# Moving the down-weight loads of a 32-expert MoE layer from SyncE's queue to GpSimd's

## The reference

```python
logits = h @ w_router + b_router                 # 32 experts
top_val, top_idx = lax.top_k(logits, 4)          # each row goes to 4 of them
gates = softmax(top_val)
...
gu = xblk @ w_gate_up[e] + b_gate_up[e]          # (rows, 1024) @ (1024, 2048)
x_glu, x_lin = split(gu); clamp both to 7
act = x_glu * sigmoid(1.702 * x_glu) * (x_lin + 1)
y = act @ w_down[e] + b_down[e]                  # (rows, 1024) @ (1024, 1024)
x[row] += gate * y
```

## Time and profile before

| | before |
|---|---|
| median of 3 runs | 1299.44 us (1299.43 to 1299.75) |
| profiled execution, its own time | 1303.46 us |
| span of the profiled execution | 1301.6 us |
| TensorE busy | 1231.7 us, 95% of the span |
| DMA, share of 16 engines, queue of SyncE (q1) | 80.0% of the span, 428.65 MB |
| DMA, queue of GpSimd (q0) | 0.6%, 3.08 MB |
| mean granted TensorE clock | 0.975 of full speed |

### The profile page before, as it was taken

The page is one execution under the profiler, slowest core; times in us unless marked ns, Lnnn a source line. Parts: engine busy times, 40 slices in busy tenths (PEclk is TensorE's granted clock), DMA queues, the critical chain, the costliest instruction groups (busy, mean ns, idle before and its releaser), DMA issues.

```text
span 1301.6 us, 15662 instructions
## 1 busy us (share of the span) xinstructions
PE 1231.7 (95%) x5923; PEld 596.5 (46%) x5923; DVE 396.1 (30%) x777; ACT 210.9 (16%) x394; POOL 78.6 (6%) x81
## 2 busy tenths in 40 slices
PE   6999979998999999999999999999999999998996
PEld 3666669856543434434343434434343443433342
DVE  3989633224342121321212121321212212121214
ACT  2134435223001101010110100001000000100002
POOL 1100144154000000000000000000000000000000
PEclk9989989798899999999999999999999999999998
DMA  9411210016999999999999999899999999999994
GB/s 378 167 69 70 87 25 2 9 49 260 397 382 421 420 422 422 422 422 422 422 422 422 422 422 422 355 361 420 422 422 421 422 422 421 421 422 420 421 422 176
DMA packets 62149, 433.69 MB, mean 333 GB/s; under 512 B 7744, under 2 KB 8128, under 8 KB 11968
## 3 DMA queue, kind: packets, MB, share of 16 engines
q1 hardware_dynamic: 59696, 428.65, 80.0%
q0 software_dynamic: 800, 3.08, 0.6%
q10 hardware_dynamic: 1616, 1.45, 0.3%
HBM read 428.50 MB, written 4.65 MB: 333 GB/s over the span
## 4 chain that ended last, share of the span: by engine, by line
PE 70%; DMA 19%; SPq 6%; DVE 2%; issue 1%; ACT 0%; ACTq 0%
PE bank L1718 20%; DMA ring<-in_w_gate_up 19%; PE bank L1738 12%; PE bank L1383 10%; SPq L431 6%; PE bank L1686 5%; PE bank L1700 5%; PE bank L1611 3%; PE bank L1813 2%; PE bank L1487 1%; PE bank L1846 1%; PE bank L1705 1%; PE bank L1728 1%; PE bank L1512 1%; PE bank L1510 1%
## 5 line engine op out<-in xcount | busy, mean ns | idle before, releaser
L1718 PE MATMUL bank<-ring,win 128*64 128x512 f32 x1984 | 442.8, 595 | 24.8 <-DMA ring<-in_w_gate_up 23.9
L1718 PEld LDWEIGHTS bank<-ring,win 128*64 128x64 f32 x1984 | 137.7, 137 | 313.7 <-issue 229.4
L1229 DVE TENSOR_SCALAR win<-bank 128x512 f32<-128x512 f32 x33 | 22.8, 691 | 683.9 <-PE bank L1718 649.7
L1738 PE MATMUL bank<-ring,win 128*64 128x512 f32 x992 | 222.2, 601 | 0.0
L1738 PEld LDWEIGHTS bank<-ring,win 128*64 128x64 f32 x992 | 69.1, 138 | 139.8 <-issue 138.1
L1686 PEld LDWEIGHTS bank<-win,qkvc 128*128 128x128 f32 x816 | 96.5, 196 | 13.9 <-issue 12.6
L1686 PE MATMUL bank<-win,qkvc 128*128 128x128 f32 (+1 forms) x816 | 100.6, 282 | 1.2 <-DVE win L1122 1.2
L787 ACT ACTIVATE win<-win 128x512 f32<-128x512 f32 x33 | 20.8, 630 | 486.9 <-DVE win L1229 486.9
L1700 PE MATMUL bank<-win 128*128 128x512 f32 (+1 forms) x204 | 95.0, 601 | 2.3 <-DVE xt L1223 1.5
L793 ACT ACTIVATE win<-bank 64x512 f32<-64x512 f32 x64 | 37.9, 591 | 286.9 <-PE bank L1738 272.8
L1223 DVE TENSOR_TENSOR xt<-xt,bank 128x512 f32<-128x512 f32 x108 | 67.8, 679 | 2.1 <-PE bank L1700 2.1
(11 more groups left out here) (281 smaller groups left out, 928.0 us busy)
## 6 DMA issues: line engine op xcount, KB each, us to landing
ring<-in_w_gate_up SPq DMA_DIRECT2D x256, 1024.0 KB, 24.5
ring<-in_w_down SPq DMA_DIRECT2D x128, 1024.0 KB, 22.3
win<-in_w_in SPq DMA_DIRECT2D x3, 2048.0 KB, 7.3
ring<-in_w_in SPq DMA_DIRECT2D x2, 2048.0 KB, 13.6
win<-in_w_out SPq DMA_DIRECT2D x2, 2048.0 KB, 8.4
win<-in_w_in SPq DMA_DIRECT2D x4, 512.0 KB, 10.5
out_ss<-ring POOLq DMA_DIRECT2D x1, 2048.0 KB, 9.3
hT<-in_xT SPq DMA_DIRECT2D x2, 768.0 KB, 6.8
```

The source lines that it names most:

```text
L1718: mm = pe.matmul(bank[half][a * BLK:(a + 1) * BLK], xs[:, k], ring[:, c:c + 512], start=False, stop=(k == KD - 1), skip_group_check=True)
L1738: mm = pe.matmul(bank[7][a * BLK:(a + 1) * BLK], actT[:, (k % 4) * P + (k // 4) * BLK:][:, 0:BLK], ring[:, c:c + 512], start=(k == 0), sto ...
```

## The change

The body that issues loads becomes functions of the issuing engine and of a set of ranks. SyncE calls `stream(sp, range(KD))` and so issues ranks 0 to 7; GpSimd calls `stream(pool, range(KD, NSLOT))` after its last instruction and so issues ranks 8 to 11. Each load keeps the slot, size, source and semaphores that it had and the wait that it had. GpSimd also loads the expert numbers from the same table.

```diff
+        def load_first(ld, ranks):
+
+            for r in [x for x in FIRST_ORDER if x in ranks]:
+                s = SLOT_OF[r]
+                if s == 10:
+                    ld.wait_ge(s_bsplit, 1)
+                if s == 0:
+                    ld.wait_ge(s_s, NB + 2)
+                if s == 2:
+                    ld.wait_ge(s_ssout, 16)
+                load_slot(ld, 0, r)
...
+        def load_expert(ld, ranks, e, value):
+
+            for r in ranks:
+                ld.wait_ge(s_wu, value(r))
+                load_slot(ld, e, r)
+
+        def stream(ld, ranks):
+
+            load_first(ld, ranks)
+            if 0 in ranks:
+                ld.dma_start(bd, b_down).then_inc(s_bd, 16)
+            load_expert(ld, ranks, 1, lambda s: USED[s])
+            ld.wait_ge(s_tabs, 1)
+            with ld.Fori(2, NE - 3) as e:
+                number = ld.value_load(expert_no[0:1, bass.ds(e, 1)], min_val=0, max_val=NE - 1)
+                load_expert(ld, ranks, number, lambda s: e * USES + (USED[s] - USES))
...
             sp.wait_ge(s_dec, NB)
...
-            load_expert(sp, 0, None)
-            sp.dma_start(bd, b_down).then_inc(s_bd, 16)
-            load_expert(sp, 1, lambda s: USED[s])
...
+            stream(sp, range(KD))
...
             pool.tensor_tensor(braw[2 * NE:3 * NE, :], braw[2 * NE:3 * NE, :], bparts[2 * NE:3 * NE], ALU.subtract)\
                 .then_inc(s_brest, 1)
+
+            pool.wait_ge(s_conf, CC)
+            pool.wait_ge(s_stq, 32)
+            pool.wait_ge(s_oTd, NT)
+            pool.wait_ge(s_ve, NT)
+            pool.wait_ge(s_sout, 16)
+            stream(pool, range(KD, NSLOT))
```

More of the change, by code:

```diff
@@ L375, in stream_step, with load_slot @@
         block = ctx.enter_context(nc.Block())
+        def load_first(ld, ranks):
[8 more added lines that the diff above has]
+                load_slot(ld, 0, r)
+        def load_slot(ld, e, r):
+            s = SLOT_OF[r]
+            dst = ring[:, s * SLOT:(s + 1) * SLOT]
+            if r < KD:
+                src = w_gate_up[bass.ds(e, 1), r * P:(r + 1) * P, :].rearrange("a p n -> (a p) n")
+            else:
+                r0 = (r - KD) * 2 * P
+                src = w_down[bass.ds(e, 1), r0:r0 + 2 * P, :].rearrange("a (p k) n -> (a p) (k n)", p=P)
+            ld.dma_start(dst, src).then_inc(s_w[s], 16)
+        def load_expert(ld, ranks, e, value):
[11 more added lines that the diff above has]
+                load_expert(ld, ranks, number, lambda s: e * USES + (USED[s] - USES))
+            ld.wait_ge(s_tabs, 2)
+            n_extra = ld.value_load(tab[0:1, NX:NX + 1], min_val=0, max_val=NX)
+            with ld.Fori(0, NX_OUTER) as g:
+                with ld.If(g * NX_INNER < n_extra):
+                    with ld.Fori(0, NX_INNER) as i0:
+                        i = g * NX_INNER + i0
+                        with ld.If(i < n_extra):
+                            ei = ld.value_load(tab[0:1, bass.ds(i, 1)], min_val=0, max_val=NE - 1)
+                            load_expert(ld, ranks, ei, lambda s: i * USES + ((NE - 4) * USES + USED[s]))
+            for e in (NE - 3, NE - 2, NE - 1):
+                number = ld.value_load(expert_no[0:1, e:e + 1], min_val=0, max_val=NE - 1)
+                load_expert(ld, ranks, number, lambda s: n_extra * USES + ((e - 1) * USES + USED[s]))
         @block.sync
```

## The result

The changed kernel takes 1322.79 us (median of 4 runs, 1317.53 to 1324.56) against 1299.60 us (4 runs, 1299.43 to 1300.66): a ratio of 1.0164, interval 1.0148 to 1.0181, so about +21 us where +17 was forecast; the two medians by themselves are 23.2 us apart. A second set of runs of the same kernel gave 1.0146 (1.0130 to 1.0162), +19 us. Both lie inside the range given, the first median of 1322.79 close to the upper end of the forecast's own 1309 to 1323. The four runs of the changed kernel spread over 7 us, the four of before over 1.2, but 23 more runs of the kernel before, beside the first experiments, spread over 5.3 (1298.21 to 1303.54). The profiled execution is the shortest of the four: 1317.53 us with a span of 1315.8, that is 14.2 us over the 1301.6 of before.

The account below looks back on a forecast made before the run. The prediction took DMA loads at about 422 GB/s as the main bound, with TensorE the bound in between. Its terms, 8.2 + 8.2 + 0.4 = 16.8, say 17 us, on 1299.4 gave 1316.4 us; range 1301 to 1336, forecast's own 1309 to 1323.

Parts of the forecast that it names:

- the order of landing: In load-bound stretches, downs in a second queue overtake gate-ups TensorE waits for; paid at expert 16 and the end.
- Sharing by packets, half each: On the 16 DMA engines, both queues alternate packets, each getting half the bandwidth while both have work; forecast chance 0.60.
- The lag of 8.2 us in the bound stretch: Where loads bound, 3.3 of 4 downs overtake, so rank 7 lands 8.2 us later (6.7 to 9.9).
- Term 1: At expert 16, TensorE starts 8.2 us later with the ring nearer full, so the DMA engines idle longer: +8.2 us.
- Term 2: At the end, rank 7 lands near the last load, so TensorE's 30.2 us tail starts later: +8.2 us.
- Term 3: At the start, ranks 8 and 9 go out later, behind GpSimd's subtraction and state store: +0.4 us (0 to 5).
- From the profile to the median: For the whole kernel, the median of the runs was taken as 4.0 us below the profiled execution.
- SyncE's queue goes first: Rival: GpSimd's queue gets much less than half, TensorE waits for downs; 1325 to 1345 us; 0.21 together with slower transfers.
- Slower transfers: Rival: GpSimd's down loads move 3% slower, 9.2 us more, 1326 us; 0.21 together with SyncE's queue first.
- No change: Rival: loads keep issue order across queues or halves don't arise, leaving only the start's cost; 1299 to 1301 us; chance 0.10.
- Faster by better filling: Rival: two queues fill the DMA engines better, above 430 GB/s the kernel gets faster, 1293 us at 2.5%; chance 0.06.

Follow-up runs that it names:

- e2: Changed kernel, but from expert 1 on GpSimd issues all twelve loads in order of use, SyncE only expert 0's; 1.0006 of the kernel before.
- e3: Changed kernel, but from expert 1 on SyncE issues even ranks and GpSimd odd ranks; expert 0 all SyncE's; 1.0030 of the kernel before.
- e1: Changed kernel, but SyncE issues all of expert 0's loads in the old order, GpSimd the downs from expert 1 on; 1.0131 of the kernel before, repeated 1.0129.
- e4: Changed kernel with engines swapped: from expert 1 on GpSimd issues gate-ups, SyncE downs; expert 0 all SyncE's; 1.0115 of the kernel before.
- e11: Changed kernel, but GpSimd issues only ranks 10 and 11 from expert 1 on, SyncE all other loads; 1.0078 of the kernel before.
- e5: Changed kernel, but GpSimd issues the downs of experts 1 to 16 only, SyncE all other loads; 1.0062 of the kernel before.
- e10: Variant of the changed kernel with expert 0's loads on SyncE and own semaphores for GpSimd's loads; its further change and time are not given.
- e6: Changed kernel, but SyncE issues all loads up to expert 16, GpSimd the downs of experts 17 to 31; 1.0078 of the kernel before.
- e8: Changed kernel with expert 0 on SyncE, and GpSimd issuing an expert's downs only after its rank 7 has landed; 1.0559 of the kernel before.

## Why the prediction was right, and where it was off

**The cause is the order of landing**, as the prediction put it. It is shown by five kernels with the same work, the same two issuing engines and the same bytes: one queue of GpSimd's costs nothing (e2), two queues in the order of use 0.3% (e3), two queues with the downs in one of them 1.2 to 1.3% (e1, e4), and half of the overtaking somewhat more than half of it (e11).

**Sharing by packets, half each.** Right: 145 packets to 145, both at 50.8%. The Trainium skill, DMA: Bandwidth & Descriptors, section Queues, rings and completion order, says that each engine takes packets from the queues that have work in turn; the trace agrees. Its section Issuing engines are not separate DMA queues says that issuing from several engines saves only the sequencer's time. That holds for the rate (422 GB/s from one queue or two) and not for the time of this kernel.

**The lag of 8.2 us in the bound stretch.** 7.7 us measured (783.43 to 791.17). Rank 7 was said to take about 28 us, and in the rows of the chain above it takes 27.7 to 28.3; the downs were put at 7 to 17 us and take 5.1 to 23.5 with a median of 13.1. TensorE's first wait for a load in the expert loop ends at 433.70 us, where before it ended at 544.90: four experts earlier, where three were forecast. One reading of the trace was too simple: TensorE did not wait for rank 7 alone but for ranks 5, 6 and 7, half a microsecond each; the sum does not use it.

**Term 1, +8.2 at expert 16.** +8.6 in the change and +7.7 in its repeat; +6.8 in e5, where it stands alone and the time rose by 8.1.

**Term 2, +8.2 at the end.** This term is the one that was mis-sized. The tail is 22.4 and 22.6 us with one queue (e2, before), 28.8 and 29.6 in the two profiles of the change, 31.4 and 32.4 in the two of e1, 33.4 in e4 and 34.3 in e6: +6.2 to +11.7. Two things make it up. The first is the term itself, the place of the last rank 7: its matmuls began 1279.0 - 1271.4 = 7.6 us ahead of the end of the loads before, 1.5 and 0.7 us ahead in the change and its repeat, and from 0.6 ahead to 0.5 behind in e10, e6, e4 and e1, so it moved by 6.1 to 8.1 of the 8.2 us. In the first profile of the change TensorE does not wait for it at all: from 1197 us on the chain stays on TensorE. The second is the clock, for which the prediction had no term. From rank 7 to the end it takes 30.2 us before, 30.3 in the change (no wait) and its repeat (a wait of 1.1 us), but 32.0, 31.9, 33.1 and 34.3 after waits of 2.1, 3.0, 3.0 and 3.0 us (e10, e1, e4, e6).

**Term 3, +0.4 at the start.** The runs give 2.2 with overlapping intervals, not told apart from 0.4. The profiles speak for a little more than forecast: counted from the first weight load and less the idle time at expert 16, the loads end 2.0 and 2.2 us later than before in the change and its repeat, and 0.5 and 0.8 in the two of e1.

**From the profile to the median.** The forecast was carried from the profile of before to its median by a fixed 4.0 us. That step failed for the change: its profiled execution is the shortest of four, 5.3 us under the median. The other three are 4.6 to 7.0 us longer. Between the two profiled executions, counted from the first weight load, the difference is 16.8 us, the sum of the prediction; that the agreement is so close is in part luck, since there term 2 was smaller and term 3 larger than forecast. The runs say 19 to 21, and where the other 2 to 4 us come from is open. The clock behind long waits could make them, as it does in the tails above, but this is not shown: no experiment changed the clock alone. A spread of this size is also not special to the split: the runs of e2, with one queue, go from 1300.28 us at a mean granted clock of 0.979 to 1307.71 at 0.972.

**The rivals.** "SyncE's queue goes first" is refuted by 145 to 145 and by e4; that the store at 138 us had a slow path of its own is argued. "Slower transfers" is refuted by e2. "No change" would have needed loads to land in the order of issue across queues; they don't (13.1 us for the downs, where they took 22.3). "Faster by better filling" is refuted by strips that stay at 419 to 423 in the stretches bound by loads, in all kernels but e8, which is lower.

Not tried: the same split with ScalarE as second issuer, and the cost of the overtaking at an expert other than number 16.

## What to carry to other kernels

A single in-order queue is also a schedule: if the consumer uses loads in a fixed order, a second queue lets the later-used ones overtake the one that is waited for, and bandwidth that was already full gives nothing in return. The lag is free while transfers are the bound all the time; count it once where the loads stop being the bound (here at expert 16, the only such place tried) and once at the end, and read it from how far ahead of the last byte the last awaited load lands. If two queues are needed, split them in the order of use (even and odd) and not by kind.

## What the runs showed of the hardware

- Loads of 1 MB issued by GpSimd, back to back, moved at the same 422 GB/s as SyncE's (5793 packets at 101.4% in 100 us), though small packets at 138 us had looked 3% slower. An issue costs GpSimd 0.53 us.
- Two queues, one of SyncE's and one of GpSimd's, with 1 MB loads waiting in both, share the 16 engines packet by packet: 145 to 145 in 5 us of the change, 2899 to 2898 in 100 us of e3, at 422 GB/s in sum.
- In the trace of the changed kernel TensorE waited 11 times for 2.1 to 3.0 us for one load. After eight of these waits the next eight matmuls took 2.5 to 3.7 us instead of 1.94, with a granted clock of 0.50 in the window shown (672 to 674 us; 1276 to 1279 us in e6 likewise); after the other three, and after every shorter wait there and before the change, they took 1.94. The wait of 2.36 us at 671.90 thus costs 1.5 us more than itself, while the three waits of half a microsecond that each expert had before cost nothing more. The final combining, 17 us behind such a wait in e6 and 16 in e4, took 7.97 and 8.09 us against 5.40, at 0.50 (1297 to 1302 us in e6), though in e4 the eight matmuls right behind the wait had taken 1.94. Why these and not the others is open.
